# Input projection in half-depth pairs of 512 columns, and the last rounds of an index mask moved among the attention units

## The chip, the cores and the metric

The kernel runs on one core of a Trainium2 chip. The metric is the device time of one execution in microseconds (us), lower is better. The engines are TensorE (PE: matmuls, with their weight loads as PEld), VectorE (DVE), ScalarE (ACT), GpSimd (POOL) and SyncE (SP), which issues the loads of the weights. Each works through its own list in order; they meet at semaphores.

## What is computed

One hybrid layer of another kind comes first and isn't touched. Two decoder layers follow, on 256 tokens of width 1024. Of each, cut to what matters here:

```
h = x @ w_in[l]                                  # 1024 x 1892: q, k, v of A and B, indexer q, k, w, ranks of C
a_q, a_k, a_v, b_q, b_k, b_v, i_q, i_k, i_w, c_q, c_kv, c_kr = split_cols(h)
o_a = sliding_window_sink_attn(rope(a_q), rope(a_k), a_v, sinks)
score = sum over 4 indexer heads of i_w * relu(rope(i_q) . rope(i_k)); the 64 best keys of each query are kept
o_b = attention of rope(b_q), rope(b_k), b_v over the kept keys
q_c = rms_norm(c_q) @ w_uq[l];  kv_c = rms_norm(c_kv) @ w_ukv[l]
o_c = attention with q_c, kv_c and rope(c_kr)
x = layer_norm(ALPHA * x + concat(o_a, o_b, o_c) @ w_out[l])
x = layer_norm(ALPHA * x + moe_ffn(x))           # 16 experts, the best 2 of the best group of 4
```

## The kernel before

A product of float32 quality is made of three matmuls (`three`, L961): operands are split into a rounded part and a remainder, and rounded x rounded, rounded x remainder and remainder x rounded are summed in PSUM. A weight tile of 1 MB is [128, 2048]. SyncE loads it into one of three raw buffers (`load`), ScalarE writes the rounded part (`split_hi`, L1690), VectorE the remainder (`split_lo`, L2094). Tile n uses buffer n mod 3, and ScalarE waits until TensorE has used tile n - 3. Tiles of a layer are numbered from T_L on; here they are called tile 0 to tile 14.

**Projection.** The 1892 columns are taken in eight tiles of 256 columns and full depth (`L_COLS`, in the order 1024 to 1891, then 0 to 1023; the fourth is 100 wide): tiles 0 to 5, 7 and 9. Tile 6 holds the up-projection of C's queries, tile 8 that of C's keys and values. `columns(n)` (L1308) calls `cols_tile` (L967): for each half of the tokens 8 steps of depth, three matmuls each, 48 in all, into one PSUM bank; banks 0 and 1 take turns. ScalarE copies each bank into `h` (`evac_h`, L1917; semaphore `ring_free`), GpSimd rotates heads (`rope`, L882), TensorE turns them (`turns`, L1293), ScalarE copies them out (`block_out`). At the start of layer 1 the tokens of the previous layer arrive half by half, and tile 0 is worked on for one half of the tokens and then the other (L1275 to L1291).

**VectorE in that stage** (from L2402): remainders of tiles 2 to 4, statistics of the two norms (`norm_stats`, L2389), remainders of tiles 5 and 6, the normalised ranks (`cn`), the indexer's scores, then the choice of the 64 best in eight rounds (`strike_out(r)`, L2435: each finds the 8 highest of a row and overwrites them, for 256 and for 128 columns), with the remainders of tiles 7 to 10 between the rounds, then the mask from it:

```python
                split(9)
                strike_out(5)
                strike_out(6)
                strike_out(7)

                lk(dve.tensor_scalar(mask_b[:, :], pick[:, :], SEL, 1e30, ALU.is_equal, ALU.mult))
```

**Attention units.** Twelve units follow (0 to 5 of kind A, 6 to 8 of C, 9 to 11 of B; only B reads the mask). In step i TensorE makes the scores of unit i, turns the probabilities of unit i - 2 and multiplies those of unit i - 3 with the values; VectorE makes the logits of unit i (`logits`, L2117) and the output of unit i - 3 (`outs`, L2136); ScalarE copies the turned probabilities of unit i - 2 (L1720) and makes the exponentials of unit i (L1707). Idle matmuls (`keep_warm`, L1042) fill some gaps. The output projection follows.

**Experts.** Tokens are gathered by matmuls into eight banks (L1491). For each bank ScalarE writes the rounded part (`gathered`, L2019), VectorE copies 64 slots as they are (L2610) and writes the remainder (L2611). The last six of the eight stand in VectorE's list ahead of the remainder of a tile and of the first product (`product`, L2618), which TensorE waits for.

## Time and profile before

| | us |
|---|---|
| median of 3 runs | 1116.34 (1115.84 to 1121.16) |
| the profiled execution, its own time | 1116.14 |
| its span, first to last instruction | 1114.3 |
| PE busy | 1081.2 (97%) |
| PEld busy | 915.1 (82%) |
| DVE busy | 742.1 (67%) |
| ACT busy | 543.7 (49%) |
| POOL busy | 110.6 (10%) |

Times in the rows are us from the start of the span. Matmuls are pipelined: a matmul of 0.28 us may be followed by the next after 0.12, so starts are compared with starts. The granted TensorE clock is 0.997 of full speed over the span. In layer 0 the projection begins at 487.6, in layer 1 its second tile at 806.4; from 504.95 and 818.01 on the two layers run alike, 313.06 us apart.

### The profile page before, as it was taken

The numbers are of one execution on the slowest core, as the hardware profiler recorded it, in microseconds if no ns is written. First come the engines' busy times: TensorE is split into PE (matmuls) and PEld (weight loads), VectorE is DVE, ScalarE is ACT, GpSimd is POOL, SyncE is SP. The second block draws the span as 40 slices with busy tenths as digits, with TensorE's granted clock in tenths as the row PEclk, the third lists the DMA queues.
The fourth block names the chain that finished last, engine by engine and source line by source line (L and its number), as shares of the span: only waits on it lengthen the run. The fifth ranks groups of instructions, "written<-read, shape, count | busy, mean of one in ns | idle before, by whom it ended". The sixth has DMA issues, their size and how long they took to land.

```text
span 1114.3 us, 16890 instructions
## 1 busy us (share of the span) xinstructions
PE 1081.2 (97%) x6604; PEld 915.1 (82%) x6604; DVE 742.1 (67%) x1000; ACT 543.7 (49%) x712; POOL 110.6 (10%) x191
## 2 busy tenths in 40 slices
PE   8999999999999999999999999999999999999996
PEld 8999999999888888889787766777798877667765
DVE  4544635587476666658978835785869868457956
ACT  5344454574454444454753435664346725346741
POOL 3000020100000000025600000000068000000000
PEclk9999999999999999999999999999999999999998
DMA  9763443554465555543311879987354017789971
GB/s 296 225 196 114 136 151 123 162 179 152 151 201 198 191 181 198 190 121 102 136 49 49 298 246 339 370 326 266 104 174 151 2 41 256 270 331 371 358 264 38
DMA packets 122102, 214.70 MB, mean 193 GB/s; under 512 B 8882, under 2 KB 78666, under 8 KB 122032
## 3 DMA queue, kind: packets, MB, share of 16 engines
q1 hardware_dynamic: 119408, 209.38, 54.6%
q0 software_dynamic: 1312, 3.88, 1.1%
q8 instruction: 47, 0.77, 0.3%
q10 hardware_dynamic: 1312, 0.49, 0.2%
q14 instruction: 23, 0.19, 0.0%
HBM read 212.63 MB, written 1.09 MB: 192 GB/s over the span
## 4 chain that ended last, share of the span: by engine, by line
PE 75%; DVE 16%; ACT 4%; DMA 2%; issue 2%; SPq 1%; POOL 0%; ACTq 0%; DVEq 0%
PE ps L963 15%; PE ps L965 15%; PE ps L964 15%; PE ps L1104 7%; DVE wlo L2094 3%; PE ps L1103 3%; PE ps L1068 3%; PE ps L1555 2%; PE ps L999 2%; PE ps L1000 2%; PE ps L1001 2%; PE ps L1034 2%; ACT whi L1690 2%; PE ps L1053 1%; PE ps L1577 1%
## 5 line engine op out<-in xcount | busy, mean ns | idle before, releaser
L2094 DVE TENSOR_TENSOR wlo<-raw,whi 128x2048 fp32r<-128x2048 f32 (+3 forms) x145 | 315.1, 2175 | 186.3 <-ACT whi L1690 185.7
L1690 ACT ACTIVATE whi<-raw 128x2048 fp32r<-128x2048 f32 (+3 forms) x145 | 261.5, 1807 | 163.1 <-PE ps L1104 61.4
L963 PE MATMUL ps<-whi,act_both 128*128 128x256 f32 (+2 forms) x448 | 142.3, 318 | 2.4 <-DVE wlo L2094 1.3
L965 PE MATMUL ps<-whi,act_both 128*128 128x256 f32 (+2 forms) x448 | 140.2, 313 | 0.0
L964 PE MATMUL ps<-wlo,act_both 128*128 128x256 f32 (+2 forms) x448 | 140.2, 313 | 0.0
L1104 PE MATMUL ps<-act_both,whi 128*128 128x512 f32 x344 | 119.1, 396 | 0.6 <-DVE wlo L2094 0.6
L963 PE MATMUL ps<-act_both,whi 128*128 128x256 f32 x408 | 117.4, 288 | 0.0
L965 PE MATMUL ps<-act_both,wlo 128*128 128x256 f32 x408 | 115.4, 283 | 0.0
L964 PE MATMUL ps<-act_both,whi 128*128 128x256 f32 x408 | 115.4, 283 | 0.0
L2094 DVE TENSOR_TENSOR wlo<-arena,whi 128x2048 fp32r<-128x2048 f32 (+1 forms) x36 | 75.9, 2113 | 34.5 <-ACT whi L1690 34.4
L963 PEld LDWEIGHTS ps<-whi,act_both 128*128 128x128 f32 x448 | 85.2, 190 | 11.8 <-issue 3.7
L965 PEld LDWEIGHTS ps<-whi,act_both 128*128 128x128 f32 x448 | 85.3, 190 | 5.3
L964 PEld LDWEIGHTS ps<-wlo,act_both 128*128 128x128 f32 x448 | 85.3, 190 | 4.7
L828 POOL TENSOR_TENSOR small<-small 128x1 f32<-128x1 f32 x14 | 8.2, 588 | 771.2 <-DVE small L2106 488.4
L1690 ACT ACTIVATE whi<-arena 128x2048 fp32r<-128x2048 f32 (+1 forms) x36 | 63.9, 1775 | 41.8 <-DMA arena<-in_w_up 21.1
L1103 PE MATMUL ps<-act_both,wlo 128*128 128x256 f32 x301 | 83.9, 279 | 0.0
L963 PE MATMUL ps<-whi,mix_hi 128*128 128x512 f32 (+1 forms) x204 | 80.4, 394 | 1.0 <-DVE mix_lo L2468 0.5
L963 PEld LDWEIGHTS ps<-act_both,whi 128*128 128x128 f32 x408 | 78.1, 191 | 3.4 <-ACT arena L1788 1.0
L965 PE MATMUL ps<-whi,mix_lo 128*128 128x512 f32 (+1 forms) x204 | 79.4, 389 | 0.0
L964 PE MATMUL ps<-wlo,mix_hi 128*128 128x512 f32 (+1 forms) x204 | 79.3, 389 | 0.0
L964 PEld LDWEIGHTS ps<-act_both,whi 128*128 128x128 f32 x408 | 78.2, 192 | 0.0
L965 PEld LDWEIGHTS ps<-act_both,wlo 128*128 128x128 f32 x408 | 78.1, 192 | 0.0
(332 smaller groups left out, 2057.2 us busy)
## 6 DMA issues: line engine op xcount, KB each, us to landing
raw<-in_w_in SPq DMA_DIRECT2D x45, 1024.0 KB, 5.5
raw<-in_w_down SPq DMA_DIRECT2D x23, 1024.0 KB, 5.0
raw<-in_w_gu SPq DMA_DIRECT2D x22, 1024.0 KB, 5.1
raw<-in_w_out SPq DMA_DIRECT2D x12, 1024.0 KB, 4.9
raw<-in_w_gate SPq DMA_DIRECT2D x24, 512.0 KB, 5.6
raw<-in_w_up SPq DMA_DIRECT2D x24, 512.0 KB, 6.8
arena<-in_w_gate SPq DMA_DIRECT2D x20, 512.0 KB, 5.2
arena<-in_w_up SPq DMA_DIRECT2D x20, 512.0 KB, 6.4
```

The costliest lines, as they stand in the source:

```text
L963: pe.matmul(o, ah, bh, start=first, stop=False)
L964: pe.matmul(o, ah, bl, start=False, stop=False)
L965: return pe.matmul(o, al, bh, start=False, stop=last)
L999: pe.matmul(o, a, cc, start=f, stop=False)
L1000: pe.matmul(o, a, d, start=False, stop=False)
L1001: x = pe.matmul(o, b, cc, start=False, stop=g)
L1034: x = pe.matmul(o[:, i, :], u["q"][i], u["k"][i], start=True, stop=True)
L1068: x = pe.matmul(oo, pt[:, b * P:(b + 1) * P], u["v"][i][kt], start=f, stop=g)
L1103: pe.matmul(ps[:, bank + part, 0:256], wl[:, k, m], act_hi[:, k, :], start=False, stop=False)
L1104: x = pe.matmul(ps[:, bank + part, :].rearrange("p (a b) -> p a b", a=2), wh[:, k, m], act_both[:, k, :, :], start=k == 0, stop=k == KD - 1)
L1690: act.activation(whi[:, c % 3, 0:n], raw_of(c, v)[:, 0:n], ACT.Copy).then_inc(hi_made, 1)
L2094: dve.tensor_tensor(wlo[:, c % 3, 0:n], raw_of(c, v)[:, 0:n], whi[:, c % 3, 0:n].bitcast(F32), ALU.subtract)\
```

## The change

The projection takes the columns in three pairs (`L_PAIRS`: 1024 to 1535, 1536 to 1891, 0 to 511) and two single tiles (`L_SINGLES`: tiles 7 and 9, columns 512 to 767 and 768 to 1023). A pair is two tiles of half depth (4 steps) and 512 or 356 columns; its result for each half of the tokens has a bank of its own, filled in two visits (`half_columns`). ScalarE copies each half of the tokens out by itself (`evac_pair`, new semaphore `cols_half`). In layer 1 both halves of the tokens use tile 0 before tile 1 is needed, and VectorE makes the remainder of tile 1 between the last two remainders of the tokens. GpSimd rotates the five indexer heads and the eight A heads in one pass each. Both `norm_stats` come after pair 1; the remainder of tile 5 ahead of them, that of tile 7 ahead of round 1. The up-projection of C's keys comes before A's queries are turned. Rounds 5, 6 and 7 of the index mask follow the outputs of steps 2, 4 and 6 of the attention units, the mask follows step 7. The copies of 64 slots go from VectorE to ScalarE, ahead of the rounded part of each bank.

```diff
-L_COLS = [4, 5, 6, 7, 0, 1, 2, 3]
-L_WIDTHS = [min(256, IN2 - tile * 256) for tile in L_COLS]
-J_COL = [0, 1, 2, 3, 4, 5, 7, 9]
-L_SIZES = {J_UQ: 768, J_UKV: 512, J_RT: 128, **{j: KD * n for j, n in zip(J_COL, L_WIDTHS)}}
+
+L_PAIRS = [(1024, 512), (1536, IN2 - 1536), (0, 512)]
+L_SINGLES = [(7, 512, 0), (9, 768, 1)]
+L_SIZES = {J_UQ: 768, J_UKV: 512, J_RT: 128, **{2 * q + half: 4 * L_PAIRS[q][1] for q in range(3) for half in range(2)}}
...
-                for n, tile in enumerate(L_COLS):
-                    w = L_WIDTHS[n]
-                    load(t0 + J_COL[n], 0, KD * w, w_in2[l, :, :, tile * 256:tile * 256 + w])
-                    if n == 5:
-                        load(t0 + J_UQ, 0, 768, w_uq[l])
-                    if n == 6:
+                for q, (c0, w) in enumerate(L_PAIRS):
+                    for half in range(2):
+                        load(t0 + 2 * q + half, 0, 4 * w, w_in2[l, :, 4 * half:4 * half + 4, c0:c0 + w])
+                load(t0 + J_UQ, 0, 768, w_uq[l])
+                for i, (j, c0, bank) in enumerate(L_SINGLES):
+                    load(t0 + j, 0, TW, w_in2[l, :, :, c0:c0 + 256])
+                    if i == 0:
                         load(t0 + J_UKV, 0, 512, I["w_ukv_2"][l])
...
-                pool.wait_ge(ring_free, l * 8 + (N_COL + 1))
-                rope(2, 64, C_CC, C_SS, cols(IQ, 2), 0)
-                pool.wait_ge(ring_free, l * 8 + (N_COL + 2))
-                rope(3, 64, C_CC, C_SS, cols(IQ + 128, 3), 1, [(0, IK)])
+                rope(5, 64, C_CC, C_SS, cols(IQ, 5), 1, [(0, IK)], 1)
 
                 pool.wait_ge(ring_free, l * 8 + (N_COL + 4))
                 rope(1, 32, C_CC16, C_SS16, cols(CKR, 1, 32), 0)
                 pool.wait_ge(cn_var, l + 1)
                 pool.tensor_tensor(crstd[:, :], cvar[:, :], mhalf[:, :], ALU.pow).then_inc(cn_rstd, 1)
 
-                pool.wait_ge(ring_free, l * 8 + (N_COL + 5))
-                rope(4, 64, C_CC, C_SS, a_queries(0), 0)
-                pool.wait_ge(ring_free, l * 8 + (N_COL + 6))
-                rope(4, 64, C_CC, C_SS, a_queries(1), 2)
+                rope(8, 64, C_CC, C_SS, cols(AQ, 8), 2, (), 5)
...
+                def half_columns(q, half, t, each=None, rounded=None, remainders=None):
+
+                    w = L_PAIRS[q][1]
+                    n = T_L + 3 * v + 2 * q + half
+                    wh, wl = (x[:, n % 3, 0:4 * w].rearrange("p (k c) -> p k c", k=4) for x in (whi, wlo))
+                    o, m = ps[:, t, 0:w], slice(t * P, (t + 1) * P)
+                    if rounded is None:
+                        for i in range(4):
+                            k = 4 * half + i
+                            if each is not None:
+                                each(k)
+                            x = three(o, act_hi[:, k, m], act_lo[:, k, m], wh[:, i, :], wl[:, i, :], k == 0, k == KD - 1)
+                        return x
+                    rounded()
+                    for i in range(4):
+                        k = 4 * half + i
+                        pe.matmul(o, act_hi[:, k, m], wh[:, i, :], start=k == 0, stop=False)
+                        pe.matmul(o, act_hi[:, k, m], wl[:, i, :], start=False, stop=False)
+                    remainders()
+                    for i in range(4):
+                        k = 4 * half + i
+                        x = pe.matmul(o, act_lo[:, k, m], wh[:, i, :], start=False, stop=k == KD - 1)
+                    return x
...
+                    keep_warm(2, 4)
+                    turn(x_tok, 0, l * 8 - 4, first_bank=2)
+                    for half in range(2):
+                        tile_ready(T_L + half, v)
+                        for t in range(TT):
+                            if t and half == 0:
+                                keep_warm(4, 2)
+                                turn(x_tok, t, l * 8 - 4, first_bank=2)
+                            x = half_columns(0, half, t, None, lambda: pe.wait_ge(tr_hi, l * 12 + 2 * t + half - 3),
+                                             lambda: pe.wait_ge(tr_lo, l * 12 + 2 * t + half - 3))
+                            if half and t == 0:
+                                x.then_inc(cols_half, 1)
+                        x.then_inc(tile_used, 1)
...
+                def pair_columns(q, half, t):
+                    if half == 0:
+                        pe.wait_ge(ring_free, l * 8 + (N_COL + 2 * q - 1 + t))
+                    tile_ready(T_L + 2 * q + half, v)
+                    x = half_columns(q, half, t)
+                    if half and t == 0:
+                        x.then_inc(cols_half, 1)
+                    if t == 1:
+                        x.then_inc(tile_used, 1)
+
+                def columns(i):
+                    j, c0, bank = L_SINGLES[i]
+                    pe.wait_ge(ring_free, l * 8 + (N_COL + 5 + i))
+                    cols_tile(T_L + j, v, bank, 256, True)
...
-                for n in range(1, 3):
-                    columns(n)
-                columns(3, (0,))
+                for half in range(2):
+                    for t in range(TT):
+                        pair_columns(1, half, t)
                 pe.wait_ge(rope_done, l * 5 + 1)
                 turns(pairs(IQ, 2) + doubled(0))
-                columns(3, (1,))
+                pair_columns(2, 0, 0)
                 tb_wait(1)
                 for t in range(TT - 1, -1, -1):
                     w = S if t else P
...
                 ins.then_inc(idx_full, 1)
-                columns(4)
+                pair_columns(2, 0, 1)
+                pair_columns(2, 1, 0)
                 pe.wait_ge(cn_ready, l + 1)
                 turns([cn[:, t, q * P:(q + 1) * P] for q in range(3) for t in range(TT)])
-                columns(5)
+                pair_columns(2, 1, 1)
                 up_queries()
-                columns(6)
+                columns(0)
+                up_keys()
                 pe.wait_ge(rope_done, l * 5 + 2)
                 turns(pairs(AQ, 4))
-                up_keys()
-                columns(7)
+                columns(1)
...
+                def evac_pair(q, t):
+                    if t == 0:
+                        act.wait_ge(cols_half, l * 3 + q + 1)
+                    else:
+                        act.wait_ge(tile_used, l * L_TILES + (T_L + 2 * q + 2))
+                    c0, w = L_PAIRS[q]
...
                 split(2)
-                for n in range(3):
-                    evac_h(n)
-                    split(3 + n)
+                if l == 0:
+                    evac_pair(0, 0)
+                    split(3)
+                else:
+                    split(3)
+                    evac_pair(0, 0)
+                evac_pair(0, 1)
+                split(4)
+                split(5)
+                evac_pair(1, 0)
+                evac_pair(1, 1)
+                split(6)
                 block_out(0, [(iq_t, 0, 4), (one(ik_t), 4, 2)])
-                evac_h(3)
-                split(6)
...
-                evac_h(4)
+                split(7)
+                evac_pair(2, 0)
                 act.wait_ge(tb_full, l * 10 + 2)
                 act.activation(mix_hi[:, 0:3, :], banks(2, 4)[:, 0:768].rearrange("p (a b) -> p a b", b=S), ACT.Copy)\
                     .then_inc(cn_hi, 1)
-                split(7)
-                evac_h(5)
+                evac_pair(2, 1)
                 split(8)
                 act.wait_ge(tile_used, l * L_TILES + (T_L + J_UQ + 1))
                 for t in range(TT):
                     act.activation(q_c[:, t, :], ps[:, 4 + t, 0:384], ACT.Copy).then_inc(ukv_sb, 1)
                 split(9)
-                evac_h(6)
-                block_out(2, [(aq_t, 0, 8)])
+                evac_single(0)
+                split(10)
                 act.wait_ge(tile_used, l * L_TILES + (T_L + J_UKV + 1))
                 for t in range(TT):
                     act.activation(kv_c[:, t, :], ps[:, 6 + t, :], ACT.Copy).then_inc(ukv_sb, 1)
-                split(10)
+                block_out(2, [(aq_t, 0, 8)])
                 split(11)
-                evac_h(7)
+                evac_single(1)
...
                     act.wait_ge(xg_full, l * KD + k + 1)
+                    act.activation(xg_pairs[:, k, :], ps[:, k, 2 * P:2 * P + 64], ACT.Copy)
                     act.activation(xg_hi[:, k, 0:2 * P], ps[:, k, 0:2 * P], ACT.Copy).then_inc(xg_h, 1)
 
...
                 split(4)
-                dve.wait_ge(ring_free, l * 8 + (N_COL + 3))
+                split(5)
+                dve.wait_ge(ring_free, l * 8 + (N_COL + 4))
                 norm_stats(0, CQ, C_QR)
-                split(5)
                 dve.wait_ge(ring_free, l * 8 + (N_COL + 4))
...
                                   mix_hi[:, 0:3, :].bitcast(F32), ALU.subtract).then_inc(cn_lo, 1)
+                split(7)
                 strike_out(1)
-                split(7)
                 strike_out(2)
                 strike_out(3)
                 split(8)
                 strike_out(4)
                 split(9)
-                strike_out(5)
-                strike_out(6)
-                strike_out(7)
-
-                lk(dve.tensor_scalar(mask_b[:, :], pick[:, :], SEL, 1e30, ALU.is_equal, ALU.mult))
-                for o, w in ((0, S), (S, P)):
-                    lk(dve.scalar_tensor_tensor(out=mask_b[:, o:o + w], in0=mask_b[:, o:o + w], scalar=NEG,
-                                                in1=cst[:, C_MC + S - w:C_MC + S], op0=ALU.add, op1=ALU.add))
+
+                def mask():
+                    lk(dve.tensor_scalar(mask_b[:, :], pick[:, :], SEL, 1e30, ALU.is_equal, ALU.mult))
+                    for o, w in ((0, S), (S, P)):
+                        lk(dve.scalar_tensor_tensor(out=mask_b[:, o:o + w], in0=mask_b[:, o:o + w], scalar=NEG,
+                                                    in1=cst[:, C_MC + S - w:C_MC + S], op0=ALU.add, op1=ALU.add))
                 split(10)
 
                 def mix_turned(half):
...
                         outs(unit_layer(i - 3), nu + (i - 3), lk)
+                    if i in (2, 4, 6):
+                        strike_out(4 + i // 2)
+                    if i == 7:
+                        mask()
                     if i == U_PER:
                         mix_turned(0)
...
                     dve.wait_ge(xg_h, l * KD + k + 1)
-                    dve.tensor_copy(xg_pairs[:, k, :], ps[:, k, 2 * P:2 * P + 64])
                     dve.tensor_tensor(xg_lo[:, k, 0:2 * P], ps[:, k, 0:2 * P], xg_hi[:, k, 0:2 * P].bitcast(F32), ALU.subtract).then_inc(xg_l, 1)
 
...
                 if not last:
-                    for half in range(2):
-                        turned_lo_half(l * 3 + 2, 1, half, 2)
+                    turned_lo_half(l * 3 + 2, 1, 0, 2)
                     split_lo(T_L + 1, v + L_TILES // 3)
+                    turned_lo_half(l * 3 + 2, 1, 1, 2)
```

## Rows read from the trace of the kernel before

**Rows 1.** The page's chain that ended last, by engine.
```profile
PE 75%; DVE 16%; ACT 4%; DMA 2%; issue 2%; SPq 1%; POOL 0%; ACTq 0%; DVEq 0%
```
**Rows 2.** Busy time by stage, layer 0: length, then PE, PEld, DVE, ACT, POOL.
```profile
487.60:540.70 53.10, 53.10 (x442) 52.57 (x441) 39.81 (x101) 26.41 (x34) 29.93 (x59) 1.00 0.43 136
540.70:583.20 42.50, 39.70 (x288) 32.67 (x286) 34.68 (x71) 29.80 (x96) 9.39 (x15) 1.00 0.12 40
```
**Rows 3.** Timeline (start, us, engine, line), TensorE: matmuls 1 and 8, 1 and 22.
```profile
479.76 0.39 PE L1000 MATMUL ps<-wlo,mix_hi 128*128 128x512 f32 x1
...
481.35 0.39 PE L1001 MATMUL ps<-whi,mix_lo 128*128 128x512 f32 x1
...
508.42 0.28 PE L965 MATMUL ps<-whi,act_both 128*128 128x100 f32 x1
...
510.76 0.28 PE L965 MATMUL ps<-whi,act_both 128*128 128x100 f32 x1
```
**Rows 4.** Timeline, VectorE in layer 0: statistics, remainders, rounds, first logits.
```profile
505.78 0.43 DVE L2392 BATCH_NORM_STATS2 small<-arena 128x6 f32<-128x256 f32 x1 [1.52 <-ACT arena L1925]
...
508.06 2.29 DVE L2094 TENSOR_TENSOR wlo<-raw,whi 128x2048 fp32r<-128x2048 f32 x1
511.45 0.29 DVE L2392 BATCH_NORM_STATS2 small<-arena 128x6 f32<-128x128 f32 x1 [1.10 <-ACT arena L1925]
...
513.67 0.96 DVE L2094 TENSOR_TENSOR wlo<-raw,whi 128x768 fp32r<-128x768 f32 x1
...
532.09 2.29 DVE L2094 TENSOR_TENSOR wlo<-raw,whi 128x2048 fp32r<-128x2048 f32 x1
534.30 0.42 DVE L2439 MAX8 small<-arena 128x8 f32<-128x256 f32 x1
...
540.70 2.50 DVE L2094 TENSOR_TENSOR wlo<-raw,whi 128x2048 fp32r<-128x2048 f32 x1
543.12 0.68 DVE L2123 SCALAR_TENSOR_TENSOR pbuf<-ps,cst 128x512 f32<-128x512 f32 x1
```
**Rows 5.** Timeline, TensorE: first matmul of tile 9, what follows it, first scores.
```profile
534.84 0.28 PE L963 MATMUL ps<-whi,act_both 128*128 128x256 f32 x1
...
540.60 0.38 PE L1296 MATMUL ps<-cst,arena 128*128 128x128 f32 x2
...
541.84 0.70 PE L1026 MATMUL ps<-arena 64*128 64x256 f32 x4
```
**Rows 6.** Timeline, units 5 to 8: a wait, unit 8's logits, exponentials, copy, turn.
```profile
559.23 0.16 DVE L2141 TENSOR_TENSOR small<-small 128x2 f32<-128x2 f32 x1 [0.30 <-PE ps L1068]
...
563.32 0.69 DVE L2125 TENSOR_REDUCE small<-pbuf 128x4 f32<-128x512 f32 x1
...
564.51 0.39 ACT L1707 ACTIVATE pbuf<-pbuf,small 128x128 f32<-128x128 f32 x1
...
566.36 0.60 ACT L1720 ACTIVATE pt<-ps 128x512 f32<-128x512 f32 x1 [0.21 <-PE ps L1068]
...
567.16 0.60 PE L1053 MATMUL ps<-cst,pbuf 128*128 128x128 f32 x4
```
**Rows 7.** One line's instructions (duration ns min/median/max): small steps of the logits.
```profile
L2132 DVE TENSOR_TENSOR small<-small x12: 160/164/807, 545.2 to 869.6; 128x2 f32<-128x2 f32 x8, 128x4 f32<-128x4 f32 x4
```
**Rows 8.** Timeline, TensorE: first matmul of the second tile of layer 1.
```profile
806.40 0.38 PE L963 MATMUL ps<-whi,act_both 128*128 128x256 f32 x1 [0.75 <-DVE wlo L2094]
```
**Rows 9.** The 64-slot copies (one line's instructions), TensorE's waits for the first product.
```profile
L2610 DVE COPY arena<-ps x16: 215/215/224, 620.0 to 944.5; 128x64 f32<-128x64 f32 x16
...
635.82 0.47 PE L963 MATMUL ps<-whi,act_both 128*128 128x512 f32 x1 [0.64 <-DVE pbuf L2618]
...
947.77 0.47 PE L963 MATMUL ps<-whi,act_both 128*128 128x512 f32 x1 [0.35 <-DVE pbuf L2618]
```
**Rows 10.** Timeline, GpSimd: first and last step of rotating four A heads.
```profile
525.68 1.33 POOL L893 TENSOR_TENSOR arena<-arena,cst 128x256 f32<-128x256 f32 x1 [1.42 <-ACT arena L1925]
...
530.87 0.74 POOL L896 TENSOR_TENSOR arena<-arena 128x256 f32<-128x256 f32 x1
```

More of the change, by code:

```diff
@@ L880, in _, with rope @@
                 lk = link
-                def rope(heads, dim, cc, ss, src, last, keys=()):
+                def rope(heads, dim, cc, ss, src, last, keys=(), ready=None):
                     for t in range(TT):
+                        if ready is not None:
+                            pool.wait_ge(ring_free, l * 8 + (N_COL + ready + t))
                         x = src(t)
@@ L1004, in down_tile, with turn @@
                 x.then_inc(tile_used, 1)
-            def turn(src, t, before, by_four=False, first_bank=0):
-                for half in range(2):
+            def turn(src, t, before, by_four=False, first_bank=0, halves=(0, 1)):
+                for half in halves:
                     pe.wait_ge(tok_ready, before + 2 * t + half + 1)
@@ L1263, in _ @@
                         turn_scaled(t, True, True)
-                    tile_ready(T_L)
-                    wh, wl = (x[:, T_L % 3, :].rearrange("p (k c) -> p k c", k=KD) for x in (whi, wlo))
                     for t in range(TT):
-                        m = slice(t * P, (t + 1) * P)
-                        for k in range(KD):
-                            pe.wait_ge(k_lo, 8 + 4 * t + k // 2 + 1)
-                            x = three(ps[:, N_COL % 2, t * 256:(t + 1) * 256], act_hi[:, k, m], act_lo[:, k, m], wh[:, k, :], wl[:, k, :],
-                                      k == 0, k == KD - 1)
@@ new lines, in _ @@
+                        for half in range(2):
+                            tile_ready(T_L + half)
+                            x = half_columns(0, half, t, lambda k: pe.wait_ge(k_lo, 8 + 4 * t + k // 2 + 1))
+                            if t:
+                                x.then_inc(tile_used, 1)
+                        if t == 0:
+                            x.then_inc(cols_half, 1)
+                else:
+                    keep_warm(2, 4)
[11 more added lines that the diff above has]
+                        x.then_inc(tile_used, 1)
@@ L1332, in up_keys @@
                     x.then_inc(tile_used, 1)
-                for n in range(1, 3):
-                    columns(n)
-                columns(3, (0,))
+                for half in range(2):
+                    for t in range(TT):
+                        pair_columns(1, half, t)
                 pe.wait_ge(rope_done, l * 5 + 1)
                 turns(pairs(IQ, 2) + doubled(0))
-                columns(3, (1,))
+                pair_columns(2, 0, 0)
                 tb_wait(1)
@@ L2715, in layer @@
                 if not last:
-                    for half in range(2):
-                        turned_lo_half(l * 3 + 2, 1, half, 2)
+                    turned_lo_half(l * 3 + 2, 1, 0, 2)
                     split_lo(T_L + 1, v + L_TILES // 3)
+                    turned_lo_half(l * 3 + 2, 1, 1, 2)
             for l in range(LAYERS):
```

44 lines of the change are left out of this document (11 added, 33 removed).

## The prediction

> **What bounds the kernel now.** I read the chain of work that ended last first: three quarters of it lie on TensorE and 16% on VectorE [rows 1]. So a cut pays only where TensorE is the engine that everything waits for, and the table by stage says where that is. In the input projection of a layer TensorE is busy for 53.10 of 53.10 us; in the attention units behind it for 39.70 of 42.50 us, VectorE for 34.68 and ScalarE for 29.80 [rows 2]. The projection thus looks like pure TensorE work. The order of VectorE in the same stage shows a second bound close under it: the remainder of tile 9 is made from 532.09 to 534.38 us, 0.5 us before TensorE begins tile 9 at 534.84 (its last 256-column tile of 48 matmuls ended at 540.60), and the first logits start at 543.12, just behind three rounds of the index mask, the mask itself and the remainder of tile 10 [rows 4, 5]. VectorE was later than TensorE there: the scores had started at 541.84 and lasted 0.70 [rows 5].
>
> **The projection in pairs.** Start to start, a 512-column matmul takes 1.59/7 = 0.227 us, a 100-column one 2.34/21 = 0.111 [rows 3], a 256-column one 5.76/48 = 0.120 [rows 5]. A 356-column one isn't in the trace; between 0.120 and 0.227 by its columns it is 0.162. I take that; its bounds are 0.120 and 0.227. A layer had 336 matmuls of 256 columns and 48 of 100. It gets 96 of 512, 48 of 356 and 96 of 256. The two wide pairs save 96 x (0.240 - 0.227) = 1.25 us, the narrow one 48 x (0.120 + 0.111 - 0.162) = 3.3 us: 4.6 us of TensorE time in each layer, most of it from the tile of 100 columns.
> The row for 256 columns is 13 ns above 256 columns at 2.4 GHz, the row for 100 columns 69 ns above its own [rows 3, 5]. The Trainium skill (TensorE: Matmul & The Clock Gate, Back-to-back issue gap) puts the fixed part of a warm matmul at about 2.5 ns; by it, 144 fewer matmuls would return 0.4 us a layer and not 4.6. The trace disagrees with it, and the rows decide.
>
> **How much of the 4.6 us arrives.** The first statistics of the norms now wait for all of pair 1. TensorE starts at 487.6 [rows 2]; 48 x 0.227 + 48 x 0.162 = 18.7 brings pair 1's end to 506.3; as before from the last narrow matmul to the statistics (511.0 to 511.45, rounded up to 0.6 for the copy-out) VectorE starts at 506.9. First statistics 508.06 - 505.78 = 2.28, second with the small steps behind them 513.67 - 511.45 = 2.22 [rows 4]: 511.4, where the kernel before stood at 513.67. From there to the remainder of tile 9 its list is the same work (remainder of tile 7 and round 1 of the mask change places). It is therefore 2.2 us early, not 4.6: tile 9 is ready at 534.38 - 2.25 = 532.1. TensorE, with 4.6 us less, asks for it at 530.3 and waits 1.8 us. That wait is the new one of the change; queued behind it are tile 9's 48 matmuls, the turning of the A keys, the first scores and so all attention units. Tile 9 takes 5.76 (534.84 to 540.60), then 1.24 to the first scores and 0.70 for them [rows 5]: first logits at 540.0, 3.1 us earlier than 543.12.
>
> **The rounds among the units.** Three rounds and the mask are 540.70 - 534.30 = 6.4 us [rows 4]. Out of the old place they give nothing beyond the above: VectorE, free at 534.5 after the remainder of tile 10, now idles until 540.0. In the new place VectorE is nearly full. From the first logits to the end of those of unit 8 (563.32 + 0.69 = 564.01) it took 20.9 us, and only three starts in them waited over 0.15 us for another engine, 0.7 us together (the longest is shown) [rows 6]. So: 540.0 + 20.2 + 6.4 = 566.6, 2.6 us later than before. Some of it is absorbed: ScalarE had begun unit 8's exponentials only at 564.51 and the copy behind them at 566.36, and TensorE turned unit 8 at 567.16 [rows 6]. Now: 566.6, then 1.6 for four exponentials, 0.1, and 0.8 from that copy to the turn: 569.1, or 1.9 us late. From that turn on TensorE goes almost without a gap to the output projection, so 1.9 us stay.
> Against that, the small two-input steps of the logits, 0.16 us in the middle, were stretched in the first three units while GpSimd worked on its rotations, four of them by 1.7 us in all (the longest, 0.81 us, is shown) [rows 7]. GpSimd's copies of the C keys will now be over before the first logits; the rotation of B still meets them. Bounds: 0 and 1.7 us off; I take 0.5. The Trainium skill (SBUF — State Buffer, SBUF: two separate sides) says that a VectorE instruction with two inputs in SBUF and a GpSimd instruction that reads SBUF lock each other out for a whole instruction; the stretched rows are of that kind, the rounds of the mask, with one input, are not.
> Attention thus ends 1.9 - 0.5 = 1.4 us later in layer 0 (0.2 to 1.9).
>
> **Start of layer 1.** TensorE waited 0.75 us for the remainder of the second tile [rows 8]. In half tiles it first works on both halves of the tokens with tile 0, and the remainder of tile 1 is made before the last remainder of the tokens: the wait goes, and pair 0 ends 0.75 us early. Next late is again VectorE's list, which hangs on pair 1, so the gain is kept. Layer 1: 1.4 - 0.75 = 0.65.
>
> **The 64-slot copies move from VectorE to ScalarE.** Eight a layer, 0.215 us each [rows 9], six of them in VectorE's list before the product that TensorE waits for, 0.64 us in layer 0 and 0.35 in layer 1 [rows 9]. Six copies at the 0.14 us by which each holds up its successor are 0.8: both waits go, -1.0 us. On ScalarE the eight cost about as much ahead of a split that VectorE reaches later anyway; if that cover is gone, up to 0.8 a layer.
>
> **Edits at nothing.** SyncE loads the same bytes in as many transfers (half tiles with longer rows, the up-projections one place on); GpSimd rotates 5 and 8 heads at once; 4 heads took 531.61 - 525.68 = 5.9 us [rows 10], so 8 take at most 11.8 from the copy of pair 2 at 517.3 on, to 529.1, and TensorE asks at 529.5; ScalarE's eight copies out of PSUM stay eight, and the keys' up-projection ahead of the turning of the A queries needs a remainder ready at 532.1 - 2.3 - 1.7 = 528.1, just when TensorE comes (530.3 less 2.3 for both steps). What these two miss comes out of the 1.8 us before tile 9, and costs nothing up to there. Refilling TensorE with wide matmuls after each turning: 0.1 us, four times, in the same slack.
>
> **Sum** against the profiled execution (1116.14 us; span 1114.3; the median of the runs is 1116.34): 1.4 + 0.65 - 1.0 = +1.05, so 1117.4 us from the median. The forecast is that TensorE's 9.2 us vanish, into the wait before tile 9 and into VectorE's rounds.
>
> **Rivals.**
> (a) The rounds hide in the units. Then the first logits' 3.1 us reach the end twice: 6.2 + 0.75 + 1.0 = 8 us faster, 1108.4. For it: ScalarE and TensorE are full in the units too, and part of VectorE's time is stretching. Against: only 0.7 us of waits in 20.9. 0.14.
> (b) All 6.4 us land, slower: the rounds stand between one unit's output and the next logits, and if every later start moves with them, a layer ends 6.4 - 3.1 = 3.3 late; 6.6 - 0.75 - 1.0 = +4.9, 1121.2; with the copies also on the path in ScalarE, 1123. It decides from the point at which ScalarE's exponentials follow each logits without delay; before, they followed 0.5 us behind (unit 8) [rows 6]. 0.08.
> (c) The wide matmuls save nothing: 356 columns at the bound of 0.227 and the wide pairs at 2 x 0.120. Pair 1 then ends 3.7 us later than above, and the whole list with it: first logits 0.6 us later than before, and a layer ends 1.4 + 3.7 = 5.1 late; 10.2 less 1.75: +8.4, 1124.8. This would also be the change not doing what it says. The rule of 2.5 ns cited above points the same way. 0.04.
>
> **Chances.** Forecast 0.74, rivals 0.14, 0.08, 0.04. A measurement here can tell about 0.5%, 5.6 us. Faster by more: (a) nearly whole, 0.13; slower by more: (c) and half of (b), 0.08; within: 0.79. The forecast's own bounds (0.2 to 1.9 in each layer) give 1115.0 to 1118.4, with the copies in ScalarE's way 1120. The range reaches toward (a) and takes in (b) at its lower price: 1110.5 to 1122.
>
> **What would show it.** In the profile after: TensorE waiting 1 to 2 us for a remainder before the last 256-column tile; first logits some 3 us earlier against the start of the projection; VectorE idle 5 us before them; no waits of VectorE on TensorE in units 1 to 8; the turn of unit 8 1 to 2 us late; no wait of 0.75 at the second tile of layer 1, nor for the first product of the experts. The prediction is wrong if TensorE comes to tile 9 without waiting, or if the rounds leave the turn of unit 8 in its place.

## The result, and the profile after

The changed kernel takes 1127.31 us in the median of 6 runs (1122.38 to 1128.91), the kernel before 1115.96 (1115.30 to 1121.16). The ratio is 1.0096, with a 95% interval of 1.0080 to 1.0113: slower by 1%, where 1117.4 us had been forecast with a range up to 1122. The time lies outside the range. The profiled execution took 1127.46 us with a span of 1125.6.

The page has the cause in its busy table by 40 slices of 28.1 us each. First TensorE's busy tenths, then its granted clock in tenths:

```profile
PE   9999999999999999999898999999998999999996
...
PEclk9999999999999999999999999999999599999998
```

In the 32nd slice (872 to 900 us) the clock stands at 5 tenths. In the kernel before this row has no 5. Busy time and clock around it (length, then PE, PEld, DVE, ACT, POOL, then granted clock, DMA share, GB/s):

```profile
870.00:873.00 3.00, 1.87 (x10) 1.10 (x8) 2.79 (x11) 2.71 (x12) 0.00 (x0) 0.99 0.00 0
873.00:900.00 27.00, 26.87 (x119) 23.90 (x119) 13.99 (x35) 12.02 (x41) 0.00 (x0) 0.50 0.01 2
900.00:903.00 3.00, 3.00 (x15) 2.54 (x15) 2.35 (x3) 0.60 (x1) 0.00 (x0) 0.96 0.00 0
```

For 27 us TensorE ran at 1.2 GHz and not at 2.4. The kernel before has 181 matmuls in these 27 us, this one 119; from 888.8 on those of the kernel before belong to its output projection already, so the fair comparison is that of single units below. These are the attention units of layer 1, from the turning of unit 5's probabilities on. TensorE is busy for 26.87 of the 27 us, so the share of busy time doesn't show the loss; only the clock column does.

What went before the fall, and how the units go behind it (timeline of TensorE: start, us, engine, line; lines have moved: 1019 scores, 1307 late turns, 1046 turned probabilities, 1061 values, 1035 spare matmuls):

```profile
870.30 1.13 PE L1019 MATMUL ps<-arena 96*128 96x256 f32 x4
872.56 0.44 PE L1307 MATMUL ps<-cst,arena 128*128 128x128 f32 x2 [1.13 <-ACT arena L1961]
873.13 1.09 PE L1046 MATMUL ps<-cst,pbuf 128*128 128x128 f32 x4
...
880.02 1.23 PE L1019 MATMUL ps<-arena 64*128 64x256 f32 x4
...
884.35 1.23 PE L1019 MATMUL ps<-arena 64*128 64x256 f32 x4
```

TensorE had waited three times for half a microsecond or more within 13 us: 1.00 us at 859.50, 0.58 at 865.68, 1.13 at 871.43. All three end with something that ScalarE made. The first also stood in the kernel before (1.00 us at 861.74). The other two are new: the exponentials hang on VectorE's logits, which a round of the mask had pushed back, and ScalarE came later with them. For the third wait the rows show it: the end of a round on VectorE, the logits of unit 5 right behind it, ScalarE's exponentials of unit 5 after 1.78 us of waiting for them, and the copy that TensorE waits for (it ends at 872.50):

```profile
868.14 0.28 DVE L2477 MATCH_REPLACE8 arena<-small,arena 128x128 f32<-128x128 f32 x1
868.45 0.69 DVE L2160 SCALAR_TENSOR_TENSOR pbuf<-ps,cst 128x512 f32<-128x512 f32 x1
...
870.28 0.40 ACT L1729 ACTIVATE pbuf<-pbuf,small 128x128 f32<-128x128 f32 x1 [1.78 <-DVE small L2169]
...
871.93 0.57 ACT L1961 ACTIVATE arena<-ps 128x512 f32<-128x512 f32 x1
```

In the kernel before ScalarE began these exponentials without a wait (870.18). At the lower clock one unit takes 884.35 - 880.02 = 4.33 us. In layer 0 of the same execution, at full clock, it takes 2.34:

```profile
563.74 0.70 PE L1019 MATMUL ps<-arena 64*128 64x256 f32 x4
...
566.08 0.70 PE L1019 MATMUL ps<-arena 64*128 64x256 f32 x4
```

All else in the trace is near the forecast. Layer 0 has no fall in this execution, and there each step can be read. The pairs:

```profile
487.86 0.48 PE L956 MATMUL ps<-whi,act_both 128*128 128x512 f32 x1
...
498.86 0.32 PE L956 MATMUL ps<-whi,act_both 128*128 128x356 f32 x1
...
506.69 0.82 PE L1307 MATMUL ps<-cst,arena 128*128 128x128 f32 x6
```

48 matmuls of 512 columns in 11.00 us are 0.229 each, 48 of 356 in 7.83 are 0.163. The place before tile 9, the first scores, the first logits, the turn of unit 8, and the first matmul behind the output projection:

```profile
532.92 0.35 PE L956 MATMUL ps<-whi,act_both 128*128 128x256 f32 x1 [1.53 <-DVE wlo L2131]
...
539.98 0.70 PE L1019 MATMUL ps<-arena 64*128 64x256 f32 x4
...
540.73 0.69 DVE L2160 SCALAR_TENSOR_TENSOR pbuf<-ps,cst 128x512 f32<-128x512 f32 x1 [5.63 <-PE ps L1019]
...
568.22 0.63 PE L1046 MATMUL ps<-cst,pbuf 128*128 128x128 f32 x4 [1.00 <-ACT pt L1742]
...
600.85 0.87 PE L1007 MATMUL ps<-cst,x_tok 128*128 128x128 f32 x5
```

The wait before tile 9 is new. Tile 9 began at 534.84 before and the scores at 541.84 [rows 5]: now 1.9 us earlier. The logits began at 543.12 [rows 4]: now 2.4 us earlier. The turn of unit 8 stood at 567.16 [rows 6]: now 1.06 later. The last of these rows stood at 599.79 before, so layer 0 ends 1.06 us later, 0.27 of it from before the projection (487.86 against 487.59).

### The profile page after: what moved, and what is told of

It is laid out like the page before. It is cut to its first block, busy times and chain, and to the rows that moved or that the text cites. A ratio compares the mean times of both kernels' runs of the same rounds, so it can differ in the third digit from the quotient of the medians.

```text
span 1125.6 us, 16281 instructions
## 1 busy us (share of the span) xinstructions
PE 1086.9 (97%) x6316; PEld 909.0 (81%) x6316; DVE 738.6 (66%) x984; ACT 545.8 (48%) x728; POOL 108.8 (10%) x159
## 4 chain that ended last, share of the span: by engine, by line
PE 77%; DVE 14%; ACT 4%; DMA 2%; issue 2%; POOL 1%; SPq 0%; ACTq 0%; DVEq 0%; POOLq 0%
PE ps L956 16%; PE ps L958 15%; PE ps L957 15%; PE ps L1097 7%; PE ps L1096 3%; DVE wlo L2131 3%; PE ps L1061 2%; PE ps L1577 2%; PE ps L992 2%; PE ps L993 2%; PE ps L994 2%; PE ps L1027 2%; ACT whi L1712 2%; PE ps L1599 1%; PE ps L1046 1%
## 5 line engine op out<-in xcount | busy, mean ns | idle before, releaser
L2131 DVE TENSOR_TENSOR wlo<-raw,whi 128x2048 fp32r<-128x2048 f32 (+4 forms) x145 | 315.6, 2180 | 186.4 <-ACT whi L1712 185.8
L1712 ACT ACTIVATE whi<-raw 128x2048 fp32r<-128x2048 f32 (+4 forms) x145 | 261.7, 1807 | 170.0 <-PE ps L958 64.8
L956 PE MATMUL ps<-whi,act_both 128*128 128x512 f32 (+2 forms) x352 | 122.3, 347 | 4.0 <-DVE wlo L2131 4.0
L958 PE MATMUL ps<-whi,act_both 128*128 128x512 f32 (+2 forms) x352 | 119.8, 340 | 0.0
L957 PE MATMUL ps<-wlo,act_both 128*128 128x512 f32 (+2 forms) x352 | 119.8, 340 | 0.0
L956 PEld LDWEIGHTS ps<-act_both,whi 128*128 128x128 f32 x408 | 78.1, 191 | 3.4 <-issue 1.0
L956 PEld LDWEIGHTS ps<-whi,act_both 128*128 128x128 f32 x352 | 66.6, 189 | 15.5 <-issue 7.1
L957 PEld LDWEIGHTS ps<-act_both,whi 128*128 128x128 f32 x408 | 78.2, 192 | 0.0
L1097 PEld LDWEIGHTS ps<-act_both,whi 128*128 128x128 f32 x344 | 62.2, 188 | 12.9 <-issue 0.9
L958 PEld LDWEIGHTS ps<-whi,act_both 128*128 128x128 f32 x352 | 66.6, 189 | 7.2
```

The source lines that it names most:

```text
L956: pe.matmul(o, ah, bh, start=first, stop=False)
L957: pe.matmul(o, ah, bl, start=False, stop=False)
L958: return pe.matmul(o, al, bh, start=False, stop=last)
L1097: x = pe.matmul(ps[:, bank + part, :].rearrange("p (a b) -> p a b", a=2), wh[:, k, m], act_both[:, k, :, :], start=k == 0, stop=k == KD - 1)
L1712: act.activation(whi[:, c % 3, 0:n], raw_of(c, v)[:, 0:n], ACT.Copy).then_inc(hi_made, 1)
L2131: dve.tensor_tensor(wlo[:, c % 3, 0:n], raw_of(c, v)[:, 0:n], whi[:, c % 3, 0:n].bitcast(F32), ALU.subtract)\
```

## Experiments

Two theories stood at the start. A: the rounds open gaps in TensorE's work among the units, and the gaps are what lets the clock fall. B: the projection in pairs brings the fall, with its shorter dense stretch and its waits ahead of the units. Each kernel is timed against the kernel before on the same chip. There were three comparisons, each on another chip: the rounds alone, the changed kernel filled, the rounds where VectorE is idle and the copies alone in the first; the fills in parts and the kernel with round 4 moved too in the second; the changed kernel again, the rounds alone filled and the kernel before with fewer spare matmuls in the third. The changed kernel with and without the fill never ran on one chip.

As a fall I count a run whose mean granted clock over its span is 0.993 or less. The kernel before never had one in the 75 runs of these comparisons (lowest 0.994). This line catches long falls only. A short one, 3.4 us at half clock, takes 0.0015 off the mean, and two traces at 0.996 that count as free of a fall have one, as shown below. The kernel before may have some too: 16 of its 75 runs lie at 0.994 or 0.995, all of them at 1117.1 to 1119.4 us, and none of these has a trace.

### The rounds alone

```diff
                 split(9)
-                strike_out(5)
-                strike_out(6)
-                strike_out(7)
...
+                def mask():
...
+                    if i in (2, 4, 6):
+                        strike_out(4 + i // 2)
+                    if i == 7:
+                        mask()
```

> The kernel before with one edit: strike-out rounds 5 to 7 and the mask go among the attention units, the projection and the 64-slot copies stay as they are. Theory A (the gaps that the rounds open in TensorE's work among the units are what lets its clock fall to 1.2 GHz in layer 1): the rounds lengthen the units by what the changed kernel shows in layer 0 (start 1.86 us early, end 1.06 us late, so 2.9 us), 2 x 2.9 = 5.8 us, and the clock falls once for some 10 us more: 1116.0 + 5.8 + 10 = about 1132 us. Theory B (the projection in pairs brings the fall, with its shorter dense stretch and its two waits of 1.5 us ahead of the units): 1121.8 us with a granted clock of 0.997.

Measured: 1124.90 us, before 1115.67 (ratio 1.0096, 1.0066 to 1.0126). Three runs lie at 1122.5 to 1123.1 us with a clock of 0.996 to 0.998, the other three at 1126.7, 1131.6 and 1132.3 with 0.993, 0.986 and 0.988. So the moved rounds alone are enough for a fall, though not in each run; B isn't needed for it. (The trace is of the run at 1122.9 us, which has no fall, so where the falls of the other three lie isn't shown.) Without one they cost 7 us, more than expected: the first scores are not early here, and layer 0 ends 3.5 us late (603.27 against 599.79).

```profile
541.91 0.70 PE L1026 MATMUL ps<-arena 64*128 64x256 f32 x4
...
603.27 0.99 PE L1014 MATMUL ps<-cst,x_tok 128*128 128x128 f32 x6
```

### The gaps filled

The changed kernel, with spare matmuls ahead of the scores of four units:

```diff
+FILL = {3: 7, 5: 5, 7: 8, 10: 6}
...
+                    if i in FILL:
+                        pe.wait_ge(l_ready, nu + i - 1)
+                        fill((4, 0)[i % 2], FILL[i])
                     if i < U_PER:
                         scores(unit_layer(i), nu + i, lk)
```

> The changed kernel with spare matmuls of 256 columns put ahead of the scores of units 3, 5, 7 and 10 (7, 5, 8 and 6 of them, 0.12 us each), where TensorE waited 1.0, 0.6 to 0.9, 1.1 and 1.0 us. Nothing waits for them. Theory A: no fall, granted clock 0.997, and the time is that of the changed kernel without the fall, 1127.3 - 10.4 = about 1117 us. Theory B: the fall stays and the time is 1127 to 1128 us.

Measured: 1115.84 us, before 1115.67 (ratio 0.9997, 0.9988 to 1.0006), clock 0.997 to 0.998 in all 12 runs. By this ratio and that of the result (1.0096), 52 more matmuls make the changed kernel 11 us faster; by that of its second comparison below (1.0055), 6 us. In the place where the clock had fallen the wait is now 0.18 us and not 1.13; the start of the turn is the same:

```profile
870.29 1.22 PE L1041 MATMUL ps<-mix_hi 128*128 128x256 f32 x8
871.34 1.03 PE L1020 MATMUL ps<-arena 96*128 96x256 f32 x4
872.55 0.44 PE L1313 MATMUL ps<-cst,arena 128*128 128x128 f32 x2 [0.18 <-ACT arena L1970]
```

VectorE's rounds and its order are untouched. Only TensorE's idleness went, and the fall with it.

### Which layer, and which gap

Three kernels take parts of that fill: `if l == 1 and i in FILL`, `if l == 0 and i in FILL`, and the first condition again with `FILL = {7: 8}`.

> The changed kernel with the spare matmuls of the fill run (7, 5, 8 and 6 of 256 columns ahead of the scores of units 3, 5, 7 and 10) in layer 1 alone. Theory A with its place (the fall comes from the gaps of layer 1's own units): no fall, granted clock 0.997 to 0.998, 1116 us as with both layers filled. Rival (the fall in layer 1 is owed to what layer 0 left behind, and the fill there was what helped): the fall stays, 1127 us.

> The same spare matmuls in layer 0 alone. Theory A with its place: the fall in layer 1 stays in most runs, granted clock 0.985, 1126 to 1127 us. Rival (what layer 0 left behind): no fall, 1116 us. This run also tells how often this chip lets the clock fall where nothing is filled in layer 1.

> The changed kernel with spare matmuls in one place only: 8 of them ahead of the scores of unit 7 in layer 1, where TensorE waited 1.13 us (871.43 to 872.56) right before the granted clock fell at 872.97. If that one gap decides: no fall, 1116 to 1117 us. If it is the sum of the gaps of units 3, 5 and 7: the fall comes in some or all runs, 1120 to 1127 us.

Measured, before 1115.31 us: layer 1 filled 1117.37 (ratio 1.0025, 1.0009 to 1.0041), a fall in 1 of 12 runs. Layer 0 filled 1116.28 (1.0019, 0.9998 to 1.0040), a fall in 3 of 12. Unit 7 alone 1118.82 (1.0042, 1.0023 to 1.0061), a fall in 4 of 12. I had expected the fall in most runs with layer 0 filled and in none with layer 1 filled. Both failed, the second by one run. The profiled execution with layer 0 filled has layer 1's gaps nearly as they were (0.72, 0.57, 1.13 us), and the clock stays:

```profile
869.38 1.13 PE L1020 MATMUL ps<-arena 96*128 96x256 f32 x4
871.63 0.44 PE L1313 MATMUL ps<-cst,arena 128*128 128x128 f32 x2 [1.13 <-ACT arena L1970]
872.21 0.63 PE L1052 MATMUL ps<-cst,pbuf 128*128 128x128 f32 x4
```

So a gap of 1.13 us makes a fall likelier; it isn't enough by itself. And the single gap of unit 7 doesn't decide: with it filled the falls go on.

The profiled execution with layer 1 filled (mean clock 0.996) has a short fall, and it lies in layer 0, whose gaps are unfilled. Busy time and clock from the last part of the wait of 1.13 us at unit 7 on (the wait ends at 559.38):

```profile
558.30:559.30 1.00, 0.00 (x0) 0.00 (x0) 0.93 (x4) 1.00 (x6) 0.00 (x0) 1.00 0.00 0
559.40:561.40 2.00, 1.87 (x15) 1.66 (x16) 1.86 (x8) 1.66 (x6) 0.00 (x0) 1.00 0.00 0
561.50:564.80 3.30, 3.30 (x18) 3.30 (x17) 3.10 (x9) 1.69 (x5) 0.00 (x0) 0.50 0.00 0
564.90:568.00 3.10, 3.10 (x25) 2.43 (x24) 2.93 (x9) 2.41 (x10) 0.00 (x0) 1.00 0.01 3
```

Layer 0 had waits of 1.00, 0.90 and 1.13 us by then. So layer 0 can fall too.

The execution with layer 0 filled gives the price of the long fall, since from layer 1's first turn of the tokens to the end of its attention its code is that of the changed kernel: 794.81 to 913.05, 118.24 us, against 794.78 to 924.31, 129.53 us, with the fall. 11.3 us.

### The changed kernel again, the rounds alone filled, and the kernel before with fewer spare matmuls

The first is unaltered. The second is the kernel of the rounds alone with the fill. The third is the kernel before with one line changed, and nothing of the change in it:

```diff
-WARM = {0: 2, 1: 3, 9: 1, 10: 1, 11: 1, 12: 2}
+WARM = {}
```

> The changed kernel itself, unaltered, beside the two below on one chip: how often its clock falls here, and what it is worth where it doesn't. Theory A: falls (granted clock under 0.990) in half of the runs or more, at 1125 us and above; without one 1116.5 us (fill in both layers gave 1115.8). If the clock hardly falls here, falls in 3 of 12 runs as with layer 0 filled, and a median of 1117 us.

> The kernel before with the rounds among the units (run of the rounds alone: 1122.5 to 1123.1 us, and 1126.7 to 1132.3 us in three of six runs with a granted clock of 0.993 to 0.986), and the spare matmuls of 7, 5, 8 and 6 ahead of units 3, 5, 7 and 10 in both layers. Theory A: the falls go, all runs at 1121.5 to 1123 us; the 7 us of the rounds stay, since they are VectorE's time and not TensorE's. If the falls came of something else in the moved rounds: a third to a half of the runs at 1127 to 1132 us still.

> The kernel before with its own spare matmuls among the units taken out (2, 3, 1, 1, 1 and 2 of 512 columns at units 0, 1, 9, 10, 11 and 12), nothing of the change in it. Theory A (idle TensorE among the units is what lets the clock fall, whoever makes it idle): falls with a granted clock of 0.985 to 0.993 in a good part of the runs, 1121 to 1127 us, and 1115 us in the others. Rival (only the longer waits of 1.0 us and more count, which this makes at the start of the units alone, or the moved rounds themselves): 1115 us and 0.997 in nearly all runs.

Measured, before 1115.58 us. The changed kernel: 1123.42 us, falls in 9 of 12 runs (0.975 to 0.992, 1120.4 to 1137.5 us; the ratio without the run of 1137.5 is 1.0055, 1.0037 to 1.0073), and 1118.2 to 1119.7 us at 0.996 in the other three. The falls are thus a matter of chance from run to run. In the comparison of the result all 6 runs had one (0.983 to 0.990); 6 of 6 and 9 of 12 can't be told apart. Its profiled execution has the fall in the same place, and the windows show it begin right behind the same gap:

```profile
870.00:872.00 2.00, 1.32 (x7) 0.80 (x6) 1.90 (x7) 1.83 (x10) 0.00 (x0) 1.00 0.00 0
872.00:874.00 2.00, 1.50 (x7) 1.21 (x8) 1.83 (x10) 2.00 (x7) 0.00 (x0) 0.67 0.00 0
874.00:876.00 2.00, 2.00 (x11) 2.00 (x11) 1.81 (x5) 0.32 (x2) 0.00 (x0) 0.50 0.04 8
```

The rounds alone, filled: 1121.88 us (1121.1 to 1122.3), clock 0.997 to 0.998 in all 6. The falls are gone (the changed kernel beside it on the same chip had 9 in 12; against 3 of 6 for the rounds alone, 0 of 6 is little by itself), and 6.3 us of the rounds stay, which the expectation puts down to VectorE's time.

The kernel before with fewer spare matmuls: 1118.95 us (ratio 1.0024, 1.0009 to 1.0039), a fall in 6 of 12 runs (0.990 to 0.993, 1120.1 to 1122.2 us), and as low as 1115.2 at 0.998 without. Neither the rounds nor the pairs are in this kernel; all it has is TensorE idle among the units, 2.05 us ahead of unit 2's scores above all:

```profile
545.60 1.20 PE L1026 MATMUL ps<-arena 64*128 64x256 f32 x4 [2.05 <-DVE small L2132]
```

This execution (mean clock 0.996, 1115.3 us, so not counted as a fall) shows a short fall that begins right behind this wait:

```profile
543.60:545.60 2.00, 0.00 (x0) 0.00 (x0) 1.90 (x5) 1.88 (x4) 2.00 (x6) 1.00 0.45 119
545.70:549.00 3.30, 3.30 (x14) 2.29 (x16) 3.16 (x6) 2.13 (x10) 3.06 (x6) 0.50 0.58 236
549.10:552.10 3.00, 2.86 (x28) 2.23 (x26) 2.78 (x9) 2.91 (x10) 1.24 (x3) 1.00 0.00 0
```

In layer 1 of the same execution the same wait of 2.05 us, at 854.74, left the clock at 1.00. The rival had said 0.997 in nearly all runs. Idle TensorE among the units is the cause, whoever makes it idle. What the six counted runs did isn't traced.

### The rounds where VectorE is idle

The changed kernel with rounds 5 to 7 in VectorE's 5.6 us ahead of the first logits; a second kernel puts round 4 there as well, so that the remainder of tile 10 comes earlier:

```diff
                 split(10)
+                for r in (5, 6, 7):
+                    strike_out(r)
...
-                    if i in (2, 4, 6):
-                        strike_out(4 + i // 2)
                     if i == 7:
                         mask()
```

> The changed kernel with rounds 5 to 7 right behind split_lo(10), where VectorE stood idle for 5.5 us ahead of the first logits (535.1 to 540.7 in layer 0, 848.6 to 854.1 in layer 1); only the mask stays among the units. Three rounds are 5.2 us, so they should hide. Theory A: no fall, each layer ends some 1.2 us before the kernel before, the copies and the boundary give 1.5 us more: 1116.0 - 2.4 - 1.5 = about 1112 us. Theory B: the fall stays, about 1122 us.

> The run with rounds 5 to 7 behind split_lo(10), and round 4 moved there as well. split_lo(10) comes 1.55 us earlier, which is TensorE's wait of 1.5 us ahead of tile 9; four rounds are 6.8 us from about 533.3, so the first logits begin at 540.1 and not 540.6: 0.5 us less a layer, 1110.5 - 1.0 = about 1109.5 us. If VectorE's list only moves the wait to the first logits: 1110.5 us. No fall either way.

Measured: 1110.48 us against 1115.67 (ratio 0.9947, 0.9932 to 0.9963), and with round 4 1109.19 against 1115.31 (0.9944, 0.9926 to 0.9962). The two ratios can't be told apart. No run of either counts as a fall (lowest 0.996 and 0.995), though in layer 0 TensorE still waits 1.00 us in both, and 1.13 us in the second. Both beat the kernel before, and by the ratios the changed one (1.0096 in its first comparison, 1.0055 in its second) by more. VectorE in the first of them: three rounds from 534.84 on, and the logits wait 0.72 us:

```profile
534.84 0.41 DVE L2476 MAX8 small<-arena 128x8 f32<-128x256 f32 x1
...
539.62 0.28 DVE L2477 MATCH_REPLACE8 arena<-small,arena 128x128 f32<-128x128 f32 x1
540.62 0.69 DVE L2160 SCALAR_TENSOR_TENSOR pbuf<-ps,cst 128x512 f32<-128x512 f32 x1 [0.72 <-DVE arena L2477]
```

Layer 0 ends at 597.05 there, 2.7 us before the kernel before and 3.8 before the changed one. With round 4 moved too, TensorE goes from the turns to tile 9 without a wait:

```profile
531.19 0.36 PE L956 MATMUL ps<-whi,act_both 128*128 128x256 f32 x1
```

The first logits still begin at 540.79, behind the fourth round. The second theory of that expectation had it so: no earlier logits. TensorE's wait now stands ahead of unit 2's scores (1.13 us).

### The 64-slot copies alone

```diff
                 def gathered(k):
                     act.wait_ge(xg_full, l * KD + k + 1)
+                    act.activation(xg_pairs[:, k, :], ps[:, k, 2 * P:2 * P + 64], ACT.Copy)
...
-                    dve.tensor_copy(xg_pairs[:, k, :], ps[:, k, 2 * P:2 * P + 64])
```

> The kernel before with only the 64-slot copies moved from VectorE to ScalarE. As forecast from the wait for the first product: 1.0 us less over both layers, 1115.0 us, no fall. If the copies carry also what the layer boundary gained (the turned tokens of layer 1 came 1.57 us earlier against the end of layer 0), 1114.4 us. If they only move the wait: 1116.0 us.

Measured: 1114.12 us against 1115.67 (ratio 0.9988, 0.9978 to 0.9999): 1.5 us less by the medians, 1.3 by the ratio, with 0.1 to 2.5 in its interval. The waits that I had counted went from 0.64 to 0.18 us in layer 0 and from 0.35 [rows 9] to under 0.1 in layer 1. But there was a third which I hadn't looked for, 37 us further on, for another product made by VectorE (TensorE's waits, us in total, times, longest; the kernel before, then this one):

```profile
PE ps L1555 <- DVE pbuf L2630: 0.9, 1, 0.9
```

```profile
PE ps L1555 <- DVE pbuf L2630: 0.3, 1, 0.3
```

### All runs together

Falls are those by the mean clock (0.993 or less), so short ones don't count.

| kernel | falls | us without a fall, about |
|---|---|---|
| before | 0 of 75 | 1115.5 |
| changed | 6 of 6, 9 of 12 | 1118 to 1120 |
| changed, both layers filled | 0 of 12 | 1115.8 |
| changed, layer 1 filled | 1 of 12 | 1117.3 |
| changed, layer 0 filled | 3 of 12 | 1116.1 |
| changed, unit 7 of layer 1 filled | 4 of 12 | 1118.1 |
| rounds alone | 3 of 6 | 1122.9 |
| rounds alone, filled | 0 of 6 | 1121.9 |
| changed, rounds in the idle stretch (with round 4) | 0 of 6 (0 of 6) | 1110.5 (1109.2) |
| copies alone | 0 of 12 | 1114.1 |
| before, fewer spare matmuls | 6 of 12 | 1116.2 |

## Why the prediction was wrong

**The mechanism of the sum was right, point by point.** 356 columns take 0.163 us (forecast 0.162), 512 take 0.229 (0.227). TensorE's new wait before tile 9 is 1.53 us (1.8). VectorE idles 5.63 us ahead of the first logits (5), and waits for no other engine in units 1 to 8, as foretold. The first logits come at 540.73, 0.27 of that from the start of the projection (540.0). That sum's own terms give 539.8; 0.2 of it has no row. Counted from the start of the projection, tile 9 begins 2.2 us earlier than before (forecast 2.7) and the first logits 2.7 earlier (3.1), where TensorE saves 4.6. For both layers: the changed kernel filled stands at +0.17 us against before, the rounds alone filled at +6.3, the copies alone at -1.5, so the projection brought about 0.17 - 6.3 + 1.5 = -4.6 us of TensorE's 9.2, with the 0.75 of layer 1's second tile in it. That is a difference between comparisons on different chips and adds up parts which overlap; the projection was not run alone.

**Rounds among the units.** Layer 0 ends 0.8 us later than before, counted from the start of the projection, where 1.4 (0.2 to 1.9) was forecast; from its turns of the tokens to the end of its attention, layer 1 without a fall takes 118.24 us against 117.50 (912.79 - 795.29), 0.7 later, where 0.65 was forecast. The wait of 0.75 us at the second tile [rows 8] is gone. The stretched small steps of the logits were to give back 0.5 us: the four took 2.37 us before and 2.10 now, so 0.3. The prediction calls the rounds instructions with one input; their `MATCH_REPLACE8` steps name two.

**Copies.** Forecast -1.0 us, measured -1.5 (an interval that holds both). The step read only the waits for the first product, and not the later one of 0.9 us, of which 0.6 went.

**The sum without a fall** is thus about right: with layer 0 filled the nine runs without a fall lie 0.8 us above the kernel before (1116.1 against 1115.3), where 1.05 was forecast. The changed kernel's own three runs without a counted fall lie higher, 2.6 to 4.2 us above, at a mean clock of 0.996 where its filled form has 0.997 to 0.998. Short falls could be the difference; no trace shows it.

**The step that failed** is the one that wasn't there. Each term of the sum was taken from rows at a granted clock of 1.00, and the sum carried that clock over to a kernel in which TensorE idles more. The same paragraph that let the rounds land on VectorE said where: between one unit's output and the next logits, so that ScalarE comes later and TensorE waits. It followed that delay to the end of the layer (0.8 us) and not to the gaps that it makes in TensorE's work on the way: 1.0, 0.9, 1.1 and 1.0 us in layer 0 at units 3, 5, 7 and 10, where the kernel before had the first alone, and nothing over 0.6 behind it. As waits these gaps are within that 0.8. They cost 11.3 us when the clock follows them, and the measured 1127.3 us lie 9.9 above the forecast. None of the three rivals had it either: (b) was to be slower by rounds that land whole, and they didn't. The signs by which the prediction wanted to be judged came true in the main (the turn of unit 8 was to be 1 to 2 us late and is 1.06, or 0.8 counted from the start of the projection) while the time missed its range: none of them looked at the clock.

There were hints in the rows of before. The kernel keeps spare matmuls in the units, at those of them where TensorE would idle; taking them out, which only the later experiment showed, costs 3.4 us in the median and brings falls. The Trainium skill (TensorE: Matmul & The Clock Gate, A second HAM failure mode: psum-queue depth-cycling) tells of a kernel in which short, frequent idle spells between groups of matmuls were enough to bring the clock down. The traces here agree: no wait ahead of the long fall was over 1.13 us. What the runs add is that it is a matter of chance: with the same program on the same chip, some executions fell and some didn't.

**What stays open.** Why the long fall came in layer 1 and not in layer 0 in both profiled executions that show one, though layer 0 has the same gaps and one more; why the clock stayed low for 27 us there and for 3.4 in the two short falls; and why filling layer 0 seems to help at all (3 of 12 against 9 of 12, on another chip). Only profiled executions tell where a fall is; for the other runs it is inferred from the mean clock. Whether the pairs make falls more frequent than the rounds alone (9 of 12 against 3 of 6) can't be told from so few runs.

## What to carry to other kernels

When work is moved onto an engine that feeds TensorE, count not only what arrives at the end, but how the idle time of TensorE is spread on the way: a few waits of a microsecond within some ten can halve its clock for the 3 to 27 us that follow. Price such an edit at both clocks and read the granted clock of each stretch and of each run, since a mean over the span hides 27 us at half speed as 0.985 and 3.4 us as 0.996, and TensorE's busy share hides it wholly. Put moved work where the receiving engine is shown idle (here 5.6 us ahead of the first logits), and where gaps must stay, fill them with spare matmuls that nothing waits for.

## What was not expected of the hardware

TensorE at 2.4 GHz fell to 1.2 GHz after three waits of 1.00, 0.58 and 1.13 us within 13 us, and stayed there for 27 us though it was busy for 26.87 of them. In the execution with layer 0 filled, waits of 0.72, 0.57 and 1.13 us in the same places left the clock at 1.00, and so did 1.00, 0.90, 1.13 and 1.00 us in layer 0 of the very execution that fell in layer 1. In the kernel before, waits of 0.51, 0.49 and 1.00 us within 4.6 us at 858 to 863 left it there as well. The rise, at about 900.2 us, came at the end of the small matmuls of the attention units, just ahead of the first 512-column matmul of the output projection (900.39). But the two short falls rose again amid the units' small matmuls, at about 549.1 and 564.8 us, 3.4 us after they began. The first of them began as the wait of 2.05 us ended, the second 2 us behind a wait of 1.13. The Trainium skill (TensorE: Matmul & The Clock Gate, What's actually happening) says that the clock is throttled by default and that activity releases it; here TensorE, busy by the profile all the way, was not released for 27 us. So the busy share of a stretch doesn't tell when the clock comes back.

The granted clock over a whole execution went with its time: 0.998 at 1122.9 us, 0.993 at 1126.7, 0.988 at 1132.3 in the kernel of the rounds alone.
